# Routing and experts of a mixture-of-experts layer as one stage

## The reference: what is computed

```
def hier_moe(h, ...):                      # 1024 tokens, 4 groups of 4 experts, top 2 in the best group
    p_grp = softmax(hf @ w_grp + b_grp);  grp_p, grp = top_k(p_grp, 1)
    p_in = softmax(e_logits[arange(n_tok), grp[:, 0]]);  top_p, top_i = top_k(p_in, TOP_K)
    weights = grp_p * top_p / sum(top_p);  expert = grp * EXPERTS_PER_GROUP + top_i
    order = argsort(flat_e)                # 2048 assignments, sorted by expert
    counts = zeros((N_EXPERTS,)).at[flat_e].add(1)
    padded = (counts + MOE_BLOCK - 1) // MOE_BLOCK * MOE_BLOCK        # blocks of 128 rows
    dest = (pad_end - padded)[se] + arange(n_assign) - (cumsum(counts) - counts)[se]
    row_tok = full((n_rows,), n_tok).at[dest].set(st);  row_w = zeros((n_rows,)).at[dest].set(sw)
    x_rows = hf_with_zero_row[row_tok].reshape(n_blocks, MOE_BLOCK, d)
    y_rows = map(expert_block, (x_rows, block_e))  # (silu(gate) * up) @ w_down[e]
    y = zeros((n_tok + 1, d)).at[row_tok].add(y_rows * row_w[:, None])
...
x = x + gt2 * ffn(rms_norm(x, g_norm2) * (1.0 + sc2) + sh2)
return rms_norm(x, g_final)
```

## Time and profile before

| | |
|---|---|
| median of 3 runs | 2597.2 us (2596.54 to 2603.38) |
| profiled execution: its own time | 2592.95 us |
| profiled execution: span, first to last instruction | 2591.2 us |
| busy in the span: PE, DVE, ACT, POOL | 2267.9, 1424.7, 1008.7, 862.4 us |
| routing, from its barrier to the next | 1915 to 1948 us |
| expert loop, from its barrier to the next | 1948 to 2563 us |
| final norm | 2563 to 2591 us |
| mean granted TensorE clock | 0.918 of full speed |

### The profile page before, as it was taken

The page is one execution under the profiler, slowest core; times in us unless marked ns, Lnnn a source line. Parts: engine busy times, 40 slices in busy tenths (PEclk is TensorE's granted clock), DMA queues, the critical chain, the costliest instruction groups (busy, mean ns, idle before and its releaser), DMA issues. The chain is left out here.

```text
span 2591.2 us, 27704 instructions
## 1 busy us (share of the span) xinstructions
PE 2267.9 (88%) x10782; PEld 1843.4 (71%) x10782; DVE 1424.7 (55%) x1757; ACT 1008.7 (39%) x1263; POOL 862.4 (33%) x629
## 2 busy tenths in 40 slices
PE   6989979993899997699999959999948999999992
PEld 1278868882788886488888847778746778887882
DVE  1536542103223321588888834543347899999993
ACT  1322211111133333345444433542224666666662
POOL 5300001000235554266666631120012344444441
PEclk9989989995799998599999979999958999999996
DMA  7633243113344554433345357564237985549525
GB/s 280 220 73 98 74 171 118 49 49 111 125 147 138 142 155 117 152 98 114 110 119 134 102 161 224 169 197 142 86 153 271 367 292 148 163 147 329 174 57 162
DMA packets 254845, 397.68 MB, mean 153 GB/s; under 512 B 26934, under 2 KB 176566, under 8 KB 247932
## 3 DMA queue, kind: packets, MB, share of 16 engines
q1 hardware_dynamic: 224876, 242.26, 29.9%
q0 software_dynamic: 28112, 148.41, 18.1%
q10 hardware_dynamic: 1728, 5.25, 0.6%
HBM read 401.55 MB, written 88.67 MB: 189 GB/s over the span
## 5 line engine op out<-in xcount | busy, mean ns | idle before, releaser
L2581 DVE TENSOR_TENSOR ex_w_lo<-ex_raw,ex_w_hi 128x2048 fp32r<-128x2048 f32 x186 | 416.4, 2285 | 41.0 <-ACT ex_w_hi L2555 40.4
L2555 ACT ACTIVATE ex_w_hi<-ex_raw 128x2048 fp32r<-128x2048 f32 x182 | 337.6, 1910 | 180.4 <-DMA ex_raw<-in_w_up_dram,w_rows 93.5
L670 POOL DMA_DIRECT2D vals<-rows_stage x40 | 21.9, 548 | 438.5 <-ACT rows_stage L662 438.5
L2457 POOL DMA_INDIRECT ex_raw<-in_w_up_dram,w_rows x60 | 82.4, 1373 | 133.2 <-DVE ex_w_lo L2581 121.3
L1996 DVE TENSOR_TENSOR mo_w_lo<-mo_w,mo_w_hi 128x1024 fp32r<-128x1024 f32 x48 | 59.7, 1244 | 102.2 <-ACT mo_w_hi L1893 102.0
L882 PE MATMUL gl_u_ps<-half_hi,gl_u_w_hi 128*128 128x512 f32 x256 | 111.8, 437 | 3.5 <-ACT gl_u_exp L900 3.5
L1531 PEld LDWEIGHTS gl_lv_ps<-gl_q_level,gl_k_level 128*128 128x128 f32 x896 | 108.6, 194 | 8.5 <-issue 3.4
L2457 POOL DMA_INDIRECT ex_raw<-in_w_down_dram,w_rows x30 | 50.6, 1688 | 184.9 <-DVE ex_w_lo L2581 178.6
L1531 PE MATMUL gl_lv_ps<-gl_q_level,gl_k_level 128*128 128x64 f32 x896 | 110.7, 276 | 1.3 <-DVE gl_scores L1661 0.7
L882 PE MATMUL ml_u_ps<-half_hi,ml_u_w_hi 128*128 128x512 f32 x256 | 104.1, 407 | 8.0 <-ACT ml_u_exp L900 8.0
L2107 PE MATMUL mo_ps<-mo_branch_hi,mo_w_hi 128*128 128x512 f32 x256 | 105.6, 412 | 5.9 <-DVE mo_w_lo L1996 5.5
(11 more groups left out here) (402 smaller groups left out, 6311.4 us busy)
## 6 DMA issues: line engine op xcount, KB each, us to landing
fr_w<-in_w_mod_dram SPq DMA_DIRECT2D x12, 2048.0 KB, 9.8
ml_u_w<-in_w_in_dram SPq DMA_DIRECT2D x32, 512.0 KB, 5.2
gl_u_w<-in_w_in_dram SPq DMA_DIRECT2D x32, 512.0 KB, 5.1
vals<-rows_stage POOLq DMA_DIRECT2D x40, 256.0 KB, 2.3
ml_v<-vals SPq DMA_DIRECT2D x20, 512.0 KB, 3.9
gl_v<-vals SPq DMA_DIRECT2D x20, 512.0 KB, 3.4
qk_w<-in_w_in_dram SPq DMA_DIRECT2D x16, 512.0 KB, 4.7
rows_w<-in_w_in_dram SPq DMA_DIRECT2D x8, 1024.0 KB, 6.4
```

The source lines that it names most:

```text
L2457: pool.indirect_dma_start(out=raw[:, q, :], out_offset=None, in_=sources[q], in_offset=bass.IndirectOffsetOnAxis(ap=m.w_rows[:, q, b:b + 1 ...
L2555: act.activation(hi[:, q, h], raw[:, q, h], ACT.Copy).then_inc(hi_done[q], 1)
L2581: dve.tensor_tensor(lo[:, q, at], raw[:, q, at], hi[:, q, at].bitcast(F32), ALU.subtract)\
```

## The change

`route` and `experts` become one function and one block; the barrier between them goes. What orders them is now a semaphore `tabled`: POOL waits for 1 ahead of a `gather`, for 2 ahead of an `add`; a `load` still waits for `lo_done`. SP issues `gate2` and `g_final` right behind the first weights; DVE waits for both ahead of its loop. DVE's order changes: the weights' parts and `w_rows` come first, then `table` and `target`, then the split of expert 0's weights; `row_weight` is taken from PSUM after that. The one-hot rows are laid out expert ahead of token number, so that one scan in each partition gives the running count over the 8 tiles (`upto`); the two matmuls for ranks and totals take 16 columns and not 128. The second set of matmuls is 16 with 64 columns (both parts side by side) and not 32 with 32, and its result goes to the bank of `h_ps`; the operands lie in the tile of expert 0's third low part, which is not in use yet.

```diff
+            dve.tensor_tensor_scan(flat(upto[:, :, :]), flat(again_n[:, :, :]), flat(both[:, :, :]), 0.0,
+                                   ALU.mult, ALU.add).then_inc(ranked, 1)
+            dve.wait_ge(ranked, 1)
+            then(tt(both[:, :, :], upto[:, :, :], both[:, :, :], ALU.subtract))
...
-            then(dve.tensor_copy(tot[:, :, :], tot_ps[:, :].rearrange("p (n e) -> p n e", e=E)))
-            then(dve.memset(pre[:, 0, :], 0.0))
-            for n in range(N):
-                then(tt(pre[:, n + 1, :], pre[:, n, :], tot[:, n, :], ALU.add))
...
+            total = upto[:, :, N - 1:N].rearrange("p e a -> p (e a)")
+            pe.matmul(cum_ps, m.before[:, :], total, start=True, stop=True)
+            pe.matmul(tot_ps, m.ones[:, :], total, start=True, stop=True).then_inc(built, 1)
...
+                    last = pe.matmul(h_ps[:, 0:2 * WIDE], is_rank[:, k, n, :],
+                                     part_w[:, k, n, :, :].rearrange("p q b -> p (q b)"),
+                                     start=(k == 0 and n == 0), stop=(k == TOP_K - 1 and n == N - 1))
...
             def gather(b):
+                pool.wait_ge(tabled, 1)
                 if b >= 2:
                     pool.wait_ge(s["t_x"], b - 1)
...
+            dve.tensor_copy(table[:, :], row0[:, :]).then_inc(tabled, 1)
...
             split_lo(0, 0)
             x_lo(0)
             split_lo(0, 1)
-            dve.wait_ge(gate_loaded, 16)
+            dve.wait_ge(tables, 2)
+            then(dve.tensor_copy(row_weight[:, :], h_ps[:, 0:BLOCKS]))
+            then(tt(row_weight[:, :], row_weight[:, :], h_ps[:, WIDE:WIDE + BLOCKS], ALU.add))
+            dve.wait_ge(gate_loaded, 32)
...
-            sp.wait_ge(first[2], 16)
+            sp.dma_start(gate2[:, :], m.mod_rows[:, 3 * D:4 * D]).then_inc(gate_loaded, 16)
+            sp.dma_start(m.g_final[:, :], w["g_final"].rearrange("(a n) -> a n", a=1).partition_broadcast(P))\
+                .then_inc(gate_loaded, 16)
...
-            pool.dma_start(gf[:, :], w["g_final"].rearrange("(a n) -> a n", a=1).partition_broadcast(P))\
-                .then_inc(loaded, 16)
-            pool.wait_ge(loaded, 16)
...
-            dve.wait_ge(loaded, 16)
```

More of the change, by code:

```diff
@@ L2183, in route @@
         x = sb("rt_x", [P, N])
[L2184 to L2188, removed]
+        hots = sb("rt_hots", [P, TOP_K, GROUPS, 4, N])
+        again_n = sb("rt_again_n", [P, E, N])
+        upto = sb("rt_upto", [P, E, N])
+        both = sb("rt_both", [P, E, N])
+        base = sb("rt_base", [P, E])
         blocks = sb("rt_blocks", [P, E])
@@ L2211, in route @@
         filled = sb("rt_filled", [P, BLOCKS])
[L2212 to L2217, removed]
+        spare = lo[:, 2, :]
@@ L2225, in _ @@
+        late = lambda b, n: b >= n
+        more = lambda b: b < BLOCKS - 1
         @block.sync
@@ new lines, in _ @@
+            then(ts(blocks[:, :], count_i[:, :], 1.0, None, ALU.max))
+            then(dve.tensor_tensor_scan(ends[:, :], ones16[:, :], blocks[:, :], 0.0, ALU.mult, ALU.add))
+            then(tt(starts[:, :], ends[:, :], blocks[:, :], ALU.subtract))
+            then(dve.scalar_tensor_tensor(out=base[:, :], in0=starts[:, :], scalar=float(P), in1=cum_ps,
+                                          op0=ALU.mult, op1=ALU.add))
+            then(tt(both[:, :, :], both[:, :, :],
+                    base[:, :].rearrange("p (e a) -> p e a", a=1).to_broadcast([P, E, N]), ALU.add))
@@ new lines, in _ @@
+            then(dve.tensor_copy(where[:, :, :, :], where_i[:, :, :, :]))
+            wide = lambda ap, size: ap.rearrange("p (n a) -> p n a", a=1).to_broadcast([P, N, size])
+            along = lambda ap, size: ap.rearrange("p (a n) -> p a n", a=1).to_broadcast([P, N, size])
+            for k in range(TOP_K):
+                then(tt(hit[:, k], wide(where[:, 1, k, :], WIDE), along(which[:, :], WIDE), ALU.is_equal))
+                then(tt(in_block[:, k], hit[:, k], wide(token[:, :], WIDE), ALU.mult))
+                tt(is_rank[:, k, :, :], wide(where[:, 0, k, :], P), along(rank[:, :], P), ALU.is_equal)\
+                    .then_inc(places, 1)
@@ new lines, in _ @@
+            for k in range(TOP_K):
+                then(tt(hit[:, k], hit[:, k], wide(weight[:, k, :], WIDE), ALU.mult))
+            for k in range(TOP_K):
+                then(dve.tensor_copy(part_w[:, k, :, 0, :], hit[:, k]))
+                then(tt(part_w[:, k, :, 1, :], hit[:, k], part_w[:, k, :, 0, :].bitcast(F32), ALU.subtract))
+            dve.sem_inc(places, 1)
+            dve.wait_ge(part_built, 4)
+            then(tt(le[:, :, :], ends[:, :].rearrange("p (a e) -> p a e", a=1).to_broadcast([P, BLOCKS, E]),
+                    which[:, 0:BLOCKS].rearrange("p (b a) -> p b a", a=1).to_broadcast([P, BLOCKS, E]), ALU.is_le))
@@ new lines, in _ @@
+            then(dve.tensor_reduce(blk[:, :], le[:, :, :], AX.X, ALU.add))
+            then(ts(blk[:, :], blk[:, :], float(E - 1), None, ALU.min))
+            then(tt(again[:, 1:], blk[:, 1:], blk[:, 0:BLOCKS - 1], ALU.is_equal))
+            then(ts(again[:, :], again[:, :], float(SKIP), None, ALU.mult))
+            for q, rows in enumerate((2 * P, 2 * P, P)):
+                if q != 1:
+                    then(dve.scalar_tensor_tensor(out=row0[:, :], in0=blk[:, :], scalar=float(rows), in1=again[:, :],
+                                                  op0=ALU.mult, op1=ALU.add))
+                then(ts(w_rows[:, q, :], row0[:, :], part[:, q:q + 1], None, ALU.add))
```

339 lines of the change are left out of this document (144 added, 195 removed).

## The result

The changed kernel took 2568.4 us (median of 4 runs, 2565.08 to 2576.23), the kernel before, on the same chip, 2596.87 us (4 runs, 2592.54 to 2603.38): ratio 0.9893, interval [0.9861, 0.9924], 27.9 us less by the means, give or take 6.6. The forecast was 2581.1 us, range 2576 to 2587.5: the right sign, too small, and the time outside the range. The profiled execution took 2565.08 us (span 2563.3).

A forecast was written before the change was run, and what follows sets the result against it. PE was taken to bound most of the kernel, with gains left where PE idles, in the routing and final norm. Terms 10.9 + 1.5 + 3.7 = 16.1 us off the median 2597.2 gave 2581.1 us, range 2576 to 2587.5.

The forecast's parts named there:

- Ranks, 3.4 us: Routing's chain of ranks: with the scan, the second `is_rank` ends at 1931.1, not 1934.55, a gain of 3.4 us.
- Table and gather order, 7.5 us: Routing's end: 7.5 us gained from all that no longer lies between table and first gather, which starts at 1937.8.
- Gather quicker, 1.5 us: First gather on POOL: slips in before DVE's first product and takes 1.03, not 2.53 us; 1.5 us gained.
- The other bound, a blocked gather: First gather: waits for DVE's product until about 1940.45, ends 1 us later, and the quicker-gather term is nothing.
- Up to the first product: Gather to block 0's first product: transposes at 1942.2, products at 1946.55, a shift of 12.4 us; block 1's weights narrowly covered.
- Final norm, 3.7 us: Last stage: DVE's last product follows ACT's last factor, ending at 2583.75, not 2587.42; gain 3.7 us, bounds 2.5 and 4.2.
- POOL's two further waits for `tabled` are met at once: nothing.: POOL's gathers and adds: the two added semaphore waits cost nothing.
- Everything in the loop is released by something before it in the loop, so what starts it earlier ends it earlier by as much: Experts' loop: an earlier start passes through in full to its end, with the loop as long as before.
- the median of the runs is 2597.2, 4.25 us more, and the prediction is for a median: Whole kernel: the 16.1 us are taken from the median 2597.2, not the profiled 2592.95, giving 2581.1 us.
- both blocked ones: First gather held by DVE's product once (14.6 us saved, 2582.6; chance 0.26) or through both (11.3, 2585.9; 0.08).
- the change that does not do what it says: POOL's start hangs on something other than the table; 2590.1 us; chance 0.08, shared with other losses of that size.
- The slower one: TensorE's clock in the loop: 1.2 GHz for another 48 us loses 24 us, ending at 2605; chance 0.04.

The follow-up runs named there:

- e7: Changed kernel with DVE's three tiny `target` instructions moved behind block 0's splits, so the split starts ahead of the gather; 2570.98 us, one execution.
- e2: Changed kernel with six unused tiles put back at the program's start, so earlier stages' tiles lie where they lay before; 2573.32 us, ratio 0.9922.
- e3: The changed kernel itself once more, in five rounds, against the kernel before; 2575.44 us, ratio 0.9931.
- e12: Kernel before with the changed kernel's two waits added to POOL's loop, at each gather and add; one execution, loop 592.4 us.
- e13: Changed kernel with those two POOL waits kept only at the first gather and first add; one execution, loop 590.9 us.
- e1: Kernel before with only the six small routing tiles placed where routing begins, no instruction changed; 2595.25 us, ratio 0.9997.
- e14: Kernel before with 64 one-column matmuls added ahead of PE's first wait in the routing; 2617.8 us, one execution.
- e16: Kernel before with 32 one-column matmuls added ahead of PE's first wait in the routing; 2596.41 us, one execution.
- e18: Kernel before with 16 one-column matmuls added at each of PE's two long idle stretches of the routing; 2586.27 us, ratio 0.9979.

## Why the forecast missed

- **Ranks, 3.4 us.** Right: 3.08. The scan took 0.42 us, 0.46 with its step, as taken; of the 0.3 missing, 0.14 is `hots` (0.71 to the next instruction, for 0.57), 0.05 the matmuls, and 0.19 the reduction to `dest`, which the sum left out: it took 0.61 us in the new layout, for 0.42.
- **Table and gather order, 7.5 us.** Right: 7.4. Together 10.5 for 10.9; shifted by the 11.4 us, the cast ends at 1926.56 for a predicted 1926.1, and the gather starts at 1926.85 for 1926.4.
- **Gather quicker, 1.5 us.** Right in kind and size: 1.44 us shorter on POOL, 1.3 to the transposes. The other bound, a blocked gather, was real: e7 has it.
- **Up to the first product.** Predicted 1946.55, less 11.4 is 1935.15; it came at 1935.76. Block 1's weights were covered, as forecast.
- **Final norm, 3.7 us.** Right: 3.9 from `co_x` to the end in this pair and 3.5 over all profiles; late next is ACT with 1.6 us a tile. But 0.7 us are given back just before: from the last product of the loop to SP's request it is 12.97 us in place of 12.29 (12.7 to 13.0 in e2 and e3).
- **"POOL's two further waits for `tabled` are met at once: nothing."** Not nothing at the loop's end: POOL's last scattered add now starts 0.73 us after DVE's last `ex_y` and not 0.28. e12 and e13 show why. The kernel before with these waits added has 0.73 there, the changed kernel without them 0.28, though the semaphore was met long before: 0.45 us. All 11 profiles with the waits have 0.73, all 9 without them 0.28.
- **"Everything in the loop is released by something before it in the loop, so what starts it earlier ends it earlier by as much"; "the loop as long as before".** This step failed: it put the loop's term at nothing. Over 7 two-stage kernels with the fetches in the old places the loop is 594.1 us on the mean, over the 10 merged ones with theirs 590.0: 4.1 us, give or take 2.2 (3.2 without e1, whose 599.4 us stand alone). The order in the loop is the same, as I argued, but its transfers share the DMA engines with PE's instruction fetches, and the merging moved those. That the fetches' places change the five blocks is shown by e14, e16 and e18. How much of the 4.1 us is theirs is not shown: the merged kernel starts its loop otherwise too, its clock was at 0.50 for 2.3 us less on the mean, and e18's profile has regained only part of the five blocks and nothing clear of the loop. This cause stays open in part.
- **The range.** The terms that the change moves make 15.0 us (10.5 + 1.3 + 3.2), for 16.1 predicted; with the loop 19.1. Measured over all 16 runs of the changed code it is 21.8, give or take 2.8. That takes in the first comparison, which showed 27.9, because four executions of each are few when a profile's untouched first 1900 us alone spread over 15; the later runs alone have 20.1. A second step failed here: "the median of the runs is 2597.2, 4.25 us more, and the prediction is for a median". That median of three was high: later ones of the kernel before, of 17 to 23 executions, are 2591.6 to 2594.2, so the 4.25 us should not have been added to the profiled 2592.95 less 16.1, which is 2576.85. The changed kernel's later medians are 2573.3 and 2575.4, so its first 2568.4 was low by 5 to 7 us, and that was luck. I had built the range from the terms' bounds and these 4.25 us, and left the spread of the comparison itself out.

Of the rivals, the gather's 1.09 us, 0.3 us behind the table's cast, rules out both blocked ones and the change that does not do what it says. The slower one did not come: TensorE's granted clock in the loop rounds to 0.98 in both kernels, with 5.1 us less at 0.50 in the changed one, not 48 more.

## What to carry over

Move an indirect gather so that it starts before, not with, a long product of DVE with both inputs in SBUF: three tiny instructions ahead of the product were worth 1.8 us in the stage. Where a block waits for transfers with all queues full, its length can also hang on where the instruction fetches fall, so an edit far ahead of it can move it, here the five blocks by 2 to 3 us; compare the granted clock, and shift the fetches with a control, before explaining such a difference by the edit. And a range for a comparison of few runs must hold the spread of executions, which in this kernel was wider than any single term.

## What the runs showed of the hardware

- A POOL gather that starts 0.38 us behind DVE's split takes 2.87 us, one that starts 0.21 us ahead of it 1.09, with DVE's 4.49 us the same in both. The Trainium skill ("SBUF — State Buffer", section "Who interferes with whom") has the first to issue hold the shared port pair for the whole instruction; for POOL the runs agree (the gather ends 1.0 us after the product that was running, in e7 and in the kernel before), but DVE, second to the gather, was not held up by it either. The page counts simple copies and `tensor_scalar` among what can take the lock, which I feared for the tiny instructions: the gather in the changed kernel lay beside the end of one `TENSOR_SCALAR` (L2564) and the small sum behind it (L2565) and lost at most 0.1 us (1.09, for 0.96 to 1.03 alone).
- Tiny PE matmuls of one column took 0.43 us each in the routing (32 in 13.78 us), at a granted clock of 0.50.
- 64 of them move PE's place in its instruction stream by one 16 KB fetch (e14: 87 in the program for 86, the ones in the loop at the old places). Such a fetch took 0.96 us in the median in the loop, nine in ten under 1.2, the longest 2.36.
- A wait of POOL for a semaphore met long before still cost 0.45 us at the last scattered add (e12 and e13).
- Before the routing the same 8126 matmuls kept PE busy for 1672.96 us in one execution and 1689.08 in another (e14). The clock was at 0.50 for 288.9 us of it in the first and for 305.8 in the second; part of the 16 us is not explained by that.
